# Gate of the linear attention: the inverse of 1 + e as a power of minus one on GpSimd, in place of a reciprocal on VectorE

## The reference, cut to what matters

```python
    o = (o_intra + o_inter).transpose(0, 2, 3, 1, 4).reshape(Bsz, S, H, dv)
    o = o * lax.rsqrt(jnp.mean(o * o, axis=-1, keepdims=True) + EPS)
    o = o.reshape(Bsz, S, H * dv) * norm_w.astype(f32) * jax.nn.silu(r.astype(f32))
    ...
    mix = jnp.concatenate([y_a.reshape(Bsz, S, A_WIDTH), y_b, y_c.reshape(Bsz, S, C_WIDTH)], axis=-1)
    x = x + mix @ w_out
```

## Time and profile before

| what | value |
|---|---|
| median of 3 runs | 2359.46 us (2355.14 to 2361.32) |
| the profiled execution, its own time | 2361.71 us |
| its span | 2359.9 us, mean granted TensorE clock 0.986 |
| busy: PE, PEld, DVE, ACT, POOL | 97%, 80%, 60%, 38%, 22% of the span |
| the chain that ended last | PE 87%, DVE 6%, ACT 3%, issue 2%, POOL 1% |
| the gates | between 266 and 291 us from the span's start |

### The profile page before, as it was taken

How to read it: one execution, slowest core, us unless ns; L and a number is a source line. 1 busy time by engine, 2 the same in 40 slices (tenths; PEclk the granted TensorE clock), 3 DMA queues, 4 the chain that set the end, 5 groups by cost and what they waited for, 6 DMA issues and landing times.

```text
span 2359.9 us, 30190 instructions
## 1 busy us (share of the span) xinstructions
PE 2277.9 (97%) x11630; PEld 1885.0 (80%) x11630; DVE 1414.0 (60%) x2332; ACT 903.5 (38%) x1521; POOL 511.3 (22%) x363
## 2 busy tenths in 40 slices
PE   8989799999999998989999999999899999999998
PEld 6656588888887865669999999999676678888887
DVE  4565658889757457764665565444736776434335
ACT  4344533332334225882522222212431794323232
POOL 3332223232322110011312211211221002322221
PEclk9989899999999999999999999999999999999999
DMA  5211017555421331001333434321133102323321
GB/s 183 81 54 55 27 54 252 188 188 200 147 85 58 103 110 36 19 19 36 119 128 126 134 127 130 119 95 58 56 98 102 34 21 81 99 91 105 99 89 54
DMA packets 76250, 227.71 MB, mean 96 GB/s; under 512 B 9151, under 2 KB 12608, under 8 KB 76108
## 3 DMA queue, kind: packets, MB, share of 16 engines
q1 hardware_dynamic: 72368, 217.80, 27.7%
q0 software_dynamic: 1856, 6.07, 0.7%
q10 hardware_dynamic: 1884, 1.91, 0.3%
HBM read 220.99 MB, written 4.76 MB: 96 GB/s over the span
## 4 chain that ended last, share of the span: by engine, by line
PE 87%; DVE 6%; ACT 3%; issue 2%; POOL 1%; DMA 0%; DVEq 0%; ACTq 0%; POOLq 0%
PE psum L786 32%; PE psum L1109 25%; PE psum L755 3%; PE psum L860 3%; PE psum L1488 3%; PE psum L807 3%; PE psum L1519 2%; PE psum L880 2%; PE psum L1442 2%; PE psum L1370 1%; PE psum L1503 1%; PE psum L1133 1%; PE psum L692 1%; PE psum L1455 1%; PE psum L1329 1%
## 5 line engine op out<-in xcount | busy, mean ns | idle before, releaser
L786 PE MATMUL psum<-mix_split,weight_split 128*128 128x384 f32 (+1 forms) x3072 | 619.9, 362 | 0.0
L786 PEld LDWEIGHTS psum<-mix_split,weight_split 128*128 128x128 f32 x3072 | 555.4, 188 | 60.5 <-issue 0.2
L1109 PE MATMUL psum<-hidden,weight_split 128*128 128x512 f32 (+1 forms) x2880 | 584.5, 363 | 0.0
L1109 PEld LDWEIGHTS psum<-hidden,weight_split 128*128 128x128 f32 x2880 | 521.4, 188 | 59.8
L2517 ACT CAST weight_split<-weight_ring 128x1024 fp32r<-128x1024 f32 x269 | 277.5, 1041 | 280.9 <-PE psum L1109 221.1
L3143 POOL TENSOR_TENSOR weight_split<-weight_ring,weight_split 128x1024 fp32r<-128x1024 f32 x89 | 230.0, 2584 | 465.3 <-ACT weight_split L2517 465.1
L2012 DVE TENSOR_TENSOR hidden<-hidden_tmp,hidden 128x512 fp32r<-128x512 f32 (+1 forms) x98 | 138.5, 1416 | 318.3 <-POOL hidden_tmp L3285 318.3
L3285 POOL TENSOR_TENSOR hidden_tmp<-hidden_tmp 128x512 f32<-128x512 f32 (+1 forms) x98 | 126.0, 1287 | 587.0 <-ACT hidden L2815 586.8
L1593 DVE TENSOR_TENSOR weight_split<-weight_ring,weight_split 128x1024 fp32r<-128x1024 f32 x180 | 226.8, 1261 | 33.0 <-ACT weight_split L2517 33.0
L2809 ACT ACTIVATE hidden_tmp<-psum 128x512 f32<-128x512 f32 (+1 forms) x94 | 62.7, 667 | 469.0 <-PE psum L786 468.3
L2035 DVE SCALAR_TENSOR_TENSOR residual<-psum,modulation,residual 128x512 f32<-128x512 f32 (+3 forms) x232 | 117.7, 552 | 135.2 <-PE psum L1109 135.0
(11 more groups left out here) (349 smaller groups left out, 2917.9 us busy)
## 6 DMA issues: line engine op xcount, KB each, us to landing
weight_ring<-in_w_mlp SPq DMA_DIRECT2D x128, 512.0 KB, 3.9
weight_ring<-in_w_ff SPq DMA_DIRECT2D x64, 512.0 KB, 4.7
mod_ring<-in_w_mod SPq DMA_DIRECT2D x48, 512.0 KB, 3.8
late_ring<-in_w_mod SPq DMA_DIRECT2D x96, 256.0 KB, 3.7
weight_ring<-in_w_in SPq DMA_DIRECT2D x45, 512.0 KB, 3.8
weight_ring<-in_w_out SPq DMA_DIRECT2D x24, 512.0 KB, 3.7
weight_ring<-in_tables SPq DMA_DIRECT2D x13, 512.0 KB, 3.7
weight_ring<-in_w_v SPq DMA_DIRECT2D x8, 512.0 KB, 5.0
```

Source lines behind the costliest of these rows:

```text
L786: m = pe.matmul(psum[:, b + r, 0:hi - lo], w[:, part_w, :], moving(x, part_x, k, lo, hi), start=k == 0 and part_w + part_x == 0, stop=k == ...
L1109: mm = pe.matmul(psum[:, b + r, 0:hi - lo], w[:, part_w, :], G[:, part_x, f % (2 * GROUP), lo:hi], start=jj == 0 and part_w + part_x == 0, ...
```

## The change

POOL's addition gets a second operation, the minimum with 1e38, and is followed on POOL, still at h = g + 1, by a TENSOR_TENSOR with the operation pow, whose second input is a column of minus ones read again for each of the 512 elements. It waits for POOL's own addition by a semaphore. DVE's reciprocal at h = g + 2 goes, and the multiplication at h = g + 3 waits for POOL itself in place of DVE. The column is one more in the small table `vecs` (234 columns in place of 233), loaded at the start with the rest.

```diff
-    for name, n in [("norm1", 8), ("norm2", 8), ("final1", 8), ("gla_norm", 2), ("gla_b", 1), ("final2", 8), ("eps", 2)] + [
+    for name, n in [("norm1", 8), ("norm2", 8), ("final1", 8), ("gla_norm", 2), ("gla_b", 1), ("final2", 8), ("eps", 2), ("minus_one", 1)] + [
...
-                if h - 2 in GATES:
-                    pr = GATES.index(h - 2)
-                    x = (la, kt)[pr]
-                    ve.wait_ge(*when("gla_pool", ("gate_one", pr)))
-                    ve.reciprocal(x[:, :], x[:, :]).then_inc(*did("gla_vec", ("gate_inverse", pr)))
...
                     po.wait_ge(*when("gla_act", ("gate_exp", pr)))
-                    po.tensor_scalar(x[:, :], x[:, :], 1.0, None, ALU.add).then_inc(*did("gla_pool", ("gate_one", pr)))
+                    po.tensor_scalar(x[:, :], x[:, :], 1.0, 1e38, ALU.add, ALU.min).then_inc(*did("gla_pool", ("gate_one", pr)))
+                    po.wait_ge(*when("gla_pool", ("gate_one", pr)))
+                    po.tensor_tensor(x[:, :], x[:, :], vec("minus_one").broadcast_to([P, S]), ALU.pow).then_inc(*did("gla_pool", ("gate_inverse", pr)))
...
-                    po.wait_ge(*when("gla_vec", ("gate_inverse", pr)))
+                    po.wait_ge(*when("gla_pool", ("gate_inverse", pr)))
                     po.tensor_tensor(x[:, :], x[:, :], B_[:, 2 + pr, :], ALU.mult).then_inc(*did("gla_pool", ("gate", pr)))
...
+    put("minus_one", np.full((P, 1), -1.0, np.float32))
```

## The result

The changed kernel takes 2520.99 us (median of 4, 2519.32 to 2522.91) against 2359.93 us of the kernel before (median of 4 here): 161.1 us more. The ratio is put at 1.0686, with a 95% interval of 1.0673 to 1.0699. The direction was forecast, the size was not: 2376.0 was predicted, and the range ended at 2406.

What follows compares the result with a forecast made beforehand. The prediction took the bound to be the gates' stretch, where TensorE waits for other engines. With a pow of 11.3 us the terms, 7.95 + 8.56 = 16.5 us on the 2359.5 median, gave 2376.0 us; range 2357 to 2406.

Steps and rivals of the forecast that it cites:

- What bounds the stretch: Both gates lie where TensorE waits for other engines; time lost or won there is lost or won at the end.
- First term, W - 3.35: First gate: the pow replaces VectorE's 3.35 us reciprocal on the path, and the move is passed on whole; 7.95 us.
- W: The duration of one pow on POOL in us, put at 11.3, with floor 1.29 and ceiling 25.8.
- Second term, W - 2.74: Second gate: the pow delays POOL's low part of mix tile 1, which TensorE awaits; 8.56 us, nothing for W below 2.74.
- The rest: Minimum: nothing, at most 1.49 us per gate; wider table: nothing; lower TensorE clock at 277 to 280 us: nothing to 2 us.
- The price of a pow: On POOL: two series, each scaled by VectorE's reciprocal-to-product factor 4.86, gave 11.3 us, between 1.29 and 25.8.
- my second rival: The pow is dear: W above 25.8 us, if not in vector form or poorly coded; chance 0.11.
- The dear pow: Second rival: W above 25.8 us on POOL; at 25.8 the time would be 2405.0 us; chance 0.11.
- The covered gate: Third rival: TensorE absorbs a late first gate, leaving only the second term, 8.6 us more, 2368.1; chance 0.03.
- the cheap pow: First rival: POOL inverts by a short series, W between 1.29 and 6.6 us, so not slower; chance 0.31.
- the gain: Fourth rival: VectorE, on the path, loses 6.7 us of work, for a gain beyond 7.1 us; chance 0.02.
- What would show it: Expected trace signs: two POOL pow rows, gate product released by POOL, later logits, low part of tile 2 drawn out.

Runs made afterwards that it cites:

- the first gate alone: The changed kernel with the pow in the first gate only, the second gate keeping VectorE's reciprocal: 2438.63 us against 2359.62 for the kernel before.
- the product: The changed kernel with a product in place of the power in the same instruction, so nothing is inverted: 2356.05 us against 2359.62 for the kernel before.
- the narrower pows: The changed kernel with the pow on only the first 64 or 256 of 512 columns in both gates: 2377.74 and 2435.59 us.

## Why the prediction was wrong, point by point

- **What bounds the stretch: right.** Nothing behind the gates made up for the loss: the part of the trace behind them has the same length within 1.2 us, and in no kernel is it shorter by more than 2.8 us.
- **First term, W - 3.35: right.** With the addition and the logits counted, the first gate alone, the product and the narrower pows give it within 0.1 us. VectorE did reach the gate product early, 4.97 us after the start of the addition in place of 5.87 (the copy in front of it), and waited there for POOL with the attention behind it.
- **Second term, W - 2.74: right**, and nothing below it, as the kernel with a product shows.
- **The rest: right in kind.** The minimum cost 0.44 us on each addition, within the bound of 1.49; the clock cost 0.78 us in the stretch, within the bound of 2. TensorE's climb back to full clock behind it is in no term: from the low part of tile 1 to L999 it took 13.89 us in place of 12.87, while other traces have 12.07 to 13.88, so it can't be told from the scatter.
- **The price of a pow: the step that failed.** The scaling by VectorE's reciprocal gave 11.3 us, the runs show 81.97, or 7 times that. The ceiling failed as well: it took 20 steps at the price of a whole plain product each, and a pow is worth 64 of them (81.97 / 1.29). I had argued from the measured factor of another instruction on another engine, VectorE's reciprocal, and from counts that no row shows: two series for a power, and 20 steps for the ceiling. Nothing in the trace bounded W from above, and my second rival said so itself, yet got 0.11. With the bound of 7.1 us crossed at W = 6.6, the chances for slower should have been higher, and the range open towards several times the ceiling.
- **Rivals.** The dear pow came true. The covered gate fell: the first gate paid whole. So did the cheap pow and the gain: W is over 12 times the 6.6 us that was to decide, and even at the price of a product the stretch was only 1.87 us shorter. The rule of the Trainium skill (GPSIMD Engine Reference, engine selection), that GpSimd is about twice as slow on elementwise work with two inputs, gave 6.7 us as an estimate. It holds for the product in this trace (1.29 against 0.69 us), but a pow here is 24 times VectorE's reciprocal (81.97 against 3.35 us). The page gives the rule for additions, products and maxima; the step to an inverse was mine.
- **What would show it.** The two rows of POOL, the gate product released by POOL and the later logits came as listed. I expected VectorE's low part of tile 2 to be drawn out to the pow's end. It was not, see the last section.

## What to carry to other kernels

An operation that has no row in any trace has no upper bound either: factors from another engine are no price, so run it once by itself before it goes on a path, or leave the range open upward. Before an inverse is moved off an engine, ask what the move is worth if the new place is as cheap as it can be: here, at the price of a product, under 2 us of the stretch, on 1 of 2 gates (3.6 us by the medians, with an interval of 1.2 to 5.4, of 2360). And look at what runs beside a slow instruction first: about the same 2 us lay in the order of two instructions on GpSimd.

## What the runs showed of the hardware that was not expected

- A pow on GpSimd costs 0.37 us and 0.1594 us for each column of 128 float32 values (64, 256 and 512 columns: 10.57, 41.17, 81.97 us), for all bases and exponents tried. A product with the same operands takes 1.04 us for 512 columns.
- While a pow runs, a VectorE instruction with two inputs in SBUF (the low part of tile 2) is not held up. The timeline of DVE after, 2.8 us into the pow of 366.71 to 448.66 us:

```profile
369.48 0.69 DVE L1829 TENSOR_TENSOR mix_split<-residual,mix_split 128x512 fp32r<-128x512 f32 x1 [1.91 <-ACT mix_split L2624]
```

  and the same with a full tile of exponents, with a pow from 361.81 to 444.00 us:

```profile
364.58 0.69 DVE L1829 TENSOR_TENSOR mix_split<-residual,mix_split 128x512 fp32r<-128x512 f32 x1 [1.91 <-ACT mix_split L2624]
```

  Beside GpSimd's weight split, a subtraction of two tiles, such an instruction does stand still (2.66 against 0.68 us above). The Trainium skill (SBUF — State Buffer, "Who interferes with whom") says that the two engines share a pair of ports under an exclusive lock, and that a VectorE instruction with two SBUF inputs contends with a GpSimd instruction that reads SBUF. The trace agrees for the weight split and not for the pow; why the pow lets VectorE through was not tried. Nor was VectorE held up beside GpSimd's addition with one input, from 281.93 to 283.42 us in the kernel before:

```profile
282.38 0.70 DVE L1834 TENSOR_TENSOR mix_split<-residual,mix_split 128x512 fp32r<-128x512 f32 x1 [2.52 <-ACT mix_split L2629]
```

- An addition with a minimum took GpSimd 1.93 us and the addition alone 1.49 us, so a second operation in this TENSOR_SCALAR is not free there: 0.44 us for 512 columns.
